# Second block of a two-block forward pass: attention head by head over both streams, with the transform branch's merge units between its steps

## The reference, cut to what matters

```python
u = ada_norm(h, g_mix[l], sh2, sc2)                       # both streams
z_conv, z_cq, z_ckv, z_kr, z_four = split_mixing(u @ w_in[l])
attn = attend(q_lat, concat(k_ctx, k_lat), concat(v_ctx, v_lat))   # 8 heads, QK 96, V 64
attn_c = attend(q_ctx, k_ctx, v_ctx)                      # context stream, not in the last layer
g0, g1, g2 = split(sigmoid(u @ w_bgate + b_bgate), 3)
y = (g0 * (silu(layer_norm(conv31(z_conv))) @ w_pw + b_pw)    # convolution branch
     + g1 * (attn @ w_o_mla)                                  # attention branch
     + g2 * (fft_real(z_four) @ w_fourier + b_four)) @ w_out  # transform branch
```

## Time and profile before

| | us |
|---|---|
| median of 3 runs | 3125.01 |
| lowest to highest | 3124.36 to 3130.96 |
| the profiled execution: its time | 3125.91 |
| the profiled execution: its span | 3124.2 |

### The profile page before, as it was taken

One profiled execution on the slowest core, in us unless ns is written; L12 is line 12 of the kernel. 1 busy time (PEld: TensorE's weight loads), 2 busy tenths in 40 slices (PEclk: granted clock), 3 DMA queues, 4 the chain that ended last, 5 costly groups with the idle time before them and its releaser, 6 DMA issues.

```text
span 3124.2 us, 52116 instructions
## 1 busy us (share of the span) xinstructions
PE 2976.0 (95%) x19700; PEld 2676.8 (86%) x19700; DVE 2058.4 (66%) x3303; ACT 1372.9 (44%) x2222; POOL 139.1 (4%) x205
## 2 busy tenths in 40 slices
PE   8998998998999999999889999999999999889898
PEld 8888998887999988897568898888988889769898
DVE  4657785557777777768843365767667666775655
ACT  4554444454545432354542254222542225654444
POOL 0000000000000000010000020100201002000000
PEclk9999999998999999999899999999999999999999
DMA  6434674435665565451102344545545445215454
GB/s 230 138 108 166 233 232 156 143 104 165 203 211 181 194 219 191 168 182 57 57 30 92 105 161 157 196 151 178 177 154 204 151 150 164 89 52 191 154 185 145
DMA packets 147696, 486.16 MB, mean 156 GB/s; under 512 B 16320, under 2 KB 25792, under 8 KB 147392
## 3 DMA queue, kind: packets, MB, share of 16 engines
q1 hardware_dynamic: 126640, 407.22, 39.3%
q0 software_dynamic: 20880, 76.56, 7.1%
HBM read 482.66 MB, written 1.05 MB: 155 GB/s over the span
## 4 chain that ended last, share of the span: by engine, by line
PE 77%; DVE 12%; ACT 5%; issue 4%; DMA 2%; DVEq 0%; POOLq 0%; ACTq 0%; SPq 0%
PE bank L1795 22%; PE bank L1797 21%; PE bank L1796 21%; DVE wlo L1018 4%; ACT whi L542 3%; PE bank L1739 2%; PE bank L1740 2%; PE bank L1741 2%; DVE acc L1542 2%; DMA bbb<-in_w_ada 1%; PE bank L2012 1%; PE aux L1996 1%; DVE bbb L1088 1%; PE bank L1870 1%; DVE small L1557 1%
## 5 line engine op out<-in xcount | busy, mean ns | idle before, releaser
L1018 DVE TENSOR_TENSOR wlo<-raw,whi 128x1024 fp32r<-128x1024 f32 (+4 forms) x850 | 948.1, 1118 | 500.2 <-ACT whi L542 494.5
L1795 PE MATMUL bank<-uhi,whi 128*128 128x256 f32 (+1 forms) x4000 | 1246.9, 312 | 13.0 <-DVE wlo L1018 6.2
L1796 PE MATMUL bank<-ulo,whi 128*128 128x256 f32 (+1 forms) x4000 | 1235.5, 309 | 0.0
L1797 PE MATMUL bank<-uhi,wlo 128*128 128x256 f32 (+1 forms) x4000 | 1235.2, 309 | 0.0
L542 ACT CAST whi<-raw 128x1024 fp32r<-128x1024 f32 (+4 forms) x850 | 810.5, 961 | 308.5 <-PE bank L1797 213.1
L1795 PEld LDWEIGHTS bank<-uhi,whi 128*128 128x128 f32 x4000 | 754.8, 189 | 75.3 <-issue 19.6
L1796 PEld LDWEIGHTS bank<-ulo,whi 128*128 128x128 f32 x4000 | 755.1, 189 | 44.7 <-issue 0.2
L1797 PEld LDWEIGHTS bank<-uhi,wlo 128*128 128x128 f32 x4000 | 755.1, 189 | 44.6
L1795 PE MATMUL bank<-yhi,whi 128*128 128x256 f32 (+1 forms) x1432 | 443.9, 310 | 16.3 <-DVE wlo L1018 9.7
L1796 PE MATMUL bank<-ylo,whi 128*128 128x256 f32 (+1 forms) x1448 | 446.1, 308 | 0.0
L1797 PE MATMUL bank<-yhi,wlo 128*128 128x256 f32 (+1 forms) x1432 | 440.7, 308 | 0.0
(11 more groups left out here) (266 smaller groups left out, 2946.5 us busy)
## 6 DMA issues: line engine op xcount, KB each, us to landing
raw<-in_w_stream SPq DMA_DIRECT2D x674, 512.0 KB, 3.5
big<-in_w_ada POOLq DMA_DIRECT2D x64, 512.0 KB, 3.9
vt<-in_w_ada POOLq DMA_DIRECT2D x51, 512.0 KB, 3.7
raw<-in_w_stream SPq DMA_DIRECT2D x80, 256.0 KB, 2.8
raw<-in_w_stream SPq DMA_DIRECT2D x48, 384.0 KB, 3.2
bbb<-in_w_ada POOLq DMA_DIRECT2D x29, 512.0 KB, 4.5
raw<-in_w_stream SPq DMA_DIRECT2D x32, 192.0 KB, 2.6
raw<-in_w_stream SPq DMA_DIRECT2D x16, 128.0 KB, 2.0
```

The lines of the kernel that those rows point to most:

```text
L1018: ve.tensor_tensor(wlo[:, u % SLOTS, 0:n], raw[:, u % SLOTS, 0:n], whi[:, u % SLOTS, 0:n].bitcast(F32), ALU.subtract).then_inc(s_low, 1)
L1795: te.matmul(out_, whi[:, u % SLOTS, w], hi(k)[:, c0:c1], start=k == 0, stop=False)
L1796: te.matmul(out_, whi[:, u % SLOTS, w], lo(k)[:, c0:c1], start=False, stop=False)
L1797: ins = te.matmul(out_, wlo[:, u % SLOTS, w], hi(k)[:, c0:c1], start=False, stop=k == plan.kt[u] - 1)
```

## The change

- Attention runs once for both streams together, head by head: for each head two context steps and two latent steps in layer 0 (32 steps), two latent steps in layer 1 (16 steps). A class `Heads` keeps which step is which.
- The transform branch's 16 units of a layer (8 gates, 8 branches) leave the merge stage and become a stage `four` of their own. Gate unit m stands behind step 4(m+1) of layer 0, branch unit m behind step 4(m+1)+2; in layer 1 behind steps 2(m+1) and 2(m+1)+1. Those that would lie past the end stand behind the last step, which are the last two in either layer. The units use banks 0 and 1 in turn.
- So attention's outputs gather in bank 2 alone, now for both streams of two heads, and the split is taken once for them. Scores have two banks in place of three and run two steps ahead in place of three.
- The gate of the transform branch is made as 0.5 tanh(0.5 x + 0.5 b) + 0.5, with Tanh on ScalarE and the rest on VectorE, where the other gates keep Sigmoid. The half bias is made once a layer (`half_bias`).
- The merge stage has 32 units of the two other branches, and its last addition takes the transform branch from `big1`.
- The norm of the convolution is at steps 23 and 9 of the new count; its Silu and the split of its output stand behind the last step instead of beside one. The table of the exponential is loaded ahead of the `kv` stage instead of behind `q`.

```diff
-LN_AT = [6, 8]
+LN_AT = [23, 9]
...
-        out.append((f"bm{l}", [8, 4, 8, 4, 8, CT] * DT))
+        out.append((f"four{l}", [8, 4] * DT))
+        out.append((f"bm{l}", [8, 4, 8, CT] * DT))
...
+class Heads:
+    def __init__(self, l):
+        self.streams = (0, 1) if l < L - 1 else (1,)
+        self.per = QT * len(self.streams)
+        self.steps = H * self.per
+        self.places = {}
+        for m in range(DT):
+            first = self.per * (m + 1)
+            self.places[2 * m] = first
+            self.places[2 * m + 1] = min(first + self.per // 2, self.steps)
+    def at(self, n):
+        return n // self.per, self.streams[n % self.per // QT], n % QT
+    def units_at(self, n):
+        return [k for k, at in self.places.items() if at == n]
+    def closes(self, n):
+        return n and n % (2 * self.per) == 0
...
# ScalarE
+                def gate4(k):
+                    if k % 2 == 0:
+                        m = k // 2
+                        done(u4, k, 0, 0)
+                        if k == 0:
+                            act.wait_ge(s_hbias, l + 1)
+                        sc.activation(big1[:, m, c0:T2], pair(u4, k)[:, c0:T2], ACT.Tanh, bias=half_bias[:, m:m + 1],
+                                      scale=0.5).then_inc(read(u4, k), 1)
                 for n in range(N + 1):
                     if n < N:
-                        turned.wait(1)
-                        sc.copy(pp[:, 2 + n % 2, 0:nk], banks[6 + n % 2][:, 0:nk]).then_inc(s_pt, 1)
+                        turned2(n)
+                    for k in heads.units_at(n - 1):
+                        gate4(k)
                     if n + 2 < N:
                         exp(n + 2)
-                    if n and n % 4 == 0:
+                    if heads.closes(n):
                         head.wait(1)
-                        j = n // 4 - 1
-                        sc.copy(yhi[:, j, s * S:(s + 1) * S], banks[j % 2][:, 0:S]).then_inc(s_ahi, 1)
+                        j = n // (2 * heads.per) - 1
+                        sc.copy(yhi[:, j, c0:T2], banks[2][:, c0:T2]).then_inc(s_ahi, 1)
+                    for k in heads.units_at(n - 1):
+                        high(u4 + k + AHEAD)
...
+                sc.preload_act_table(ACT.Exp)
                 u0 = U[f"kv{l}"]
...
# VectorE
+                def branch4(k):
+                    if k % 2:
+                        m = k // 2
+                        dve.wait_ge(*after(u4 + k - 1))
+                        chained(ve.tensor_scalar(big1[:, m, c0:T2], big1[:, m, c0:T2], 0.5, 0.5, ALU.mult, ALU.add))
+                        done(u4, k, 0, 0)
+                        ve.scalar_tensor_tensor(big1[:, m, c0:T2], banks[(u4 + k) % 2][:, c0:T2], b_four[:, m:m + 1],
+                                                big1[:, m, c0:T2], ALU.add, ALU.mult).then_inc(read(u4, k), 1)
...
-                    if n + 3 < N:
-                        bias(n + 3)
-                    if n and n % 4 == 0:
+                    if n + 2 < N:
+                        bias(n + 2)
+                    for k in heads.units_at(n - 1):
+                        branch4(k)
+                    if heads.closes(n):
                         ahi.wait(1)
-                        j = n // 4 - 1
-                        rest(ylo[:, j, s * S:(s + 1) * S], banks[j % 2][:, 0:S], yhi[:, j, s * S:(s + 1) * S])
-                    if not s:
-                        conv.taps(1)
-                        continue
+                        j = n // (2 * heads.per) - 1
+                        rest(ylo[:, j, c0:T2], banks[2][:, c0:T2], yhi[:, j, c0:T2])
+                    for k in heads.units_at(n - 1):
+                        low(u4 + k + AHEAD)
...
# TensorE
-                    if n + 3 < N:
-                        scores(n + 3)
+                    if n + 2 < N:
+                        scores(n + 2)
...
+                    for k in heads.units_at(n):
+                        unit4(k)
-                split.wait(2)
+                split.wait(1)
```

More of the change, by code:

```diff
@@ L456, in _ @@
             for name, n in plan.count.items():
-                per = 12 if name.startswith("bm") else SLOTS
+                per = 8 if name.startswith("bm") else SLOTS
                 first = SLOTS if U[name] == 0 else 0
@@ L879, in attention2 @@
                         sc.preload_act_table(ACT.Exp)
[L880 to L887, removed]
+                for k in heads.units_at(N):
+                    gate4(k)
+                    high(u4 + k + AHEAD)
+                lng, lnb = p2("ln_g", l, CT), p2("ln_b", l, CT)
+                sc.preload_act_table(ACT.Silu)
+                for m in range(CT):
+                    act.wait_ge(s_scaled, CT * l + m + 1)
+                    sc.activation(ychi[:, m, c0:T2], acc[:, m, c0:T2], ACT.Silu, bias=lnb[:, m:m + 1],
+                                  scale=lng[:, m:m + 1])
+                    sc.activation(acc[:, m, c0:T2], acc[:, m, c0:T2], ACT.Silu, bias=lnb[:, m:m + 1],
+                                  scale=lng[:, m:m + 1]).then_inc(s_chigh, 1)
             for l in range(L):
@@ L2011, in outputs, with unit4 @@
                     for k in range(nk // P):
-                        ins = te.matmul(banks[hh // 2 % 2][r, qt * P:(qt + 1) * P], vt[:, k, hh * HD:(hh + 1) * HD],
+                        ins = te.matmul(banks[2][r, q0:q0 + P], vt[:, k, hh * HD:(hh + 1) * HD],
                                         pp[:, 2 + n % 2, k * P:(k + 1) * P], start=k == 0, stop=k == nk // P - 1)
-                    if n % 4 == 3:
+                    if heads.closes(n + 1):
                         ins.then_inc(s_head, 1)
-                for n in range(3):
+                def unit4(k):
+                    gate = k % 2 == 0
+                    unit(u4, k, 0, 0, lambda t: uhi[:, t, :] if gate else yhi[:, FG + t, :],
+                         lambda t: ulo[:, t, :] if gate else ylo[:, FG + t, :], c0, T2, True)
+                for n in range(2):
                     scores(n)
@@ L2029, in attention2 @@
                         ins.then_inc(s_cmean, 1)
[L2030 removed]
+                    if n == LN_AT[l] + 3:
                         for m in range(CT):
@@ L2106, in _ @@
                 aop.wait(1)
-                for s in range(c0 // S, 2):
-                    attention2(l, s)
-                rows_of = {1: (yhi, ylo, 0), 3: (yhi, ylo, 4)}
+                attention2(l)
+                pe.wait_ge(*after(U[f"bm{l}"] - 2))
                 def rows(part):
                     def at(j, k):
-                        if j % 6 == 5:
+                        if j == 1 and part == 0 and k == 0:
+                            pe.wait_ge(*after(U[f"bm{l}"] - 1))
+                        if j % 4 == 3:
                             if part == 0 and k == 0:
```

123 lines of the change are left out of this document (67 added, 56 removed).

## The result

The changed kernel takes **3071.6 us** (median of 4 runs, 3064.2 to 3086.1) against 3124.75 for the kernel before in the same comparison: a ratio of 0.9831, interval 0.9810 to 0.9852. The forecast was 3111 with a range of 3099 to 3122. The direction was right; the gain of 53 us is nearly four times the forecast of 14, and outside the range.

What follows compares the result with a forecast made beforehand. Attention was taken as a latency chain with holes, the merge stage as matmul-bound. Gains of 18.6 - 2.5 - 1.2 - 0.4 = 14.5 us, off 3125.9, gave 3111, range 3099 to 3122.

Steps and rivals of the forecast that it cites:

- the hole time: Attention stages: the change fills TensorE's idle gaps with merge units, and can win only those gaps; units' own time cancels.
- What else moves: Side effects: table load costs 1.2 us in layer 0 and 0.4 in layer 1; Tanh, weight DMAs and queues cost nothing.
- to the first transpose: Layer 0, start of attention: from the first scores to TensorE's first transpose, 4.2 us instead of 4.4.
- first four steps: Layer 0, attention steps with no unit behind them, run at the lower clock: 12.0 us.
- pass between kinds of matmul: Both layers' attention: TensorE going between attention's and a unit's matmuls and back costs 0.2 us per unit, 3.2 per layer.
- ring and norm: Layer 0 attention: VectorE and ScalarE's probability chain is late 0.2 to 0.4 us once a head; with norm, 4.0 in all.
- ring, steps 3 to 8, layer 1: VectorE and ScalarE wait on each other longer than TensorE's step while taps last: 1.0 us a step, 5.7 in all.
- seam at the merge stage's start, layer 1: Convolution's Silu, with two table loads, stands ahead of the fourth unit's conversion: about 1.0 us lost.
- moved table load: Exponential's table load, now ahead of the key and value units, comes late: 1.2 us in layer 0, 0.4 in layer 1.
- the holes close fully: Rival: no chain stalls or switching cost in either layer, gain 33 us, so 3092; chance 0.13.
- the ring reaches layer 0 too: Rival: layer 0's 14 steps with a unit each lose layer 1's 1.0 us, giving 3121; chance 0.12.
- the slower rival: Rival: attention's small matmuls between units hold TensorE's clock down, up to 3166 over layer 0 behind step 4; chance 0.05.

Runs made afterwards that it cites:

- the kernel with the bias moved: Changed kernel with `half_bias` allocated behind all other second-block tiles, so every other tile lies where it did before the change: 3107.6 us, ratio 0.9941.
- the second kernel at each: Kernel before with, at 32, weights and rows all 32 bytes further: ratio 1.0001; at 96, 32 bytes behind the weights and 32 ahead of the rows: 0.9994.

## Why the prediction was wrong, and where it was right

**The step that failed is a missing one.** The account went through the instructions and put at nothing a line of the change that issues none: the allocation of `half_bias`, which the diff in "The change" leaves out too. The prediction says "What it can win is the hole time, not the units' time", and "they cost the same in both places, so they cancel", with 0.235 and 0.119 us per matmul taken as constants of the kernel. They are constants of a placement. With the rows 32 bytes further, all unit matmuls of the program follow one another faster, from a mean of 0.1207 us to 0.1189 for 256 columns and from 0.2343 to 0.2333 for 512, moved or not. 34 us of the measured 53 came from there. Also "What else moves" looked at queues, tables and DMAs, and never at addresses.

**The other steps,** against the kernel with the bias moved, in which that effect is absent. Its 3107.6 us lie 3 from the forecast and inside the range. In part that is luck: the layers gained 24.8 us by the traces where 16.1 were forecast, while the table's load in layer 1 cost 0.9 more than forecast. By the medians of one session the reordering gives 19.5 us, against the 14.5 of the sum.

| term | forecast, us | measured |
|---|---|---|
| layer 0, attention and units | 150.1 | 145.7 |
| of it: to the first transpose | 4.2 | 4.1 |
| of it: first four steps | 12.0 | 11.4 |
| of it: pass between kinds of matmul | 3.2 | 0.8 |
| of it: ring and norm | 4.0 | 0.5 + 1.4 |
| layer 0's gain | 18.6 | 297.7 - 274.8 = 22.9 |
| layer 1, attention and units | 92.8 | 88.5 |
| of it: ring, steps 3 to 8, layer 1 | 5.7 | 4.9 |
| of it: pass between kinds of matmul | 3.2 | about 0 |
| seam at the merge stage's start, layer 1 | 1.0, at the fourth unit | 0.4 + 0.65 idle, at the fourth and fifth |
| layer 1's gain | -2.5 | 156.7 - 154.8 = 1.9 |
| moved table load | 1.2 + 0.4 | 1.3 + 1.3 |

(The gains take attention and merge stage together, from the first scores to the merge stage's end.)

The mis-sized term in both layers is the **pass** between attention's matmuls and a unit's: 0.2 us each, from one place of the first block. In layer 0 of the kernel with the bias moved, the transposes that open two successive heads stand 16.33 us apart:

```profile
1553.78 0.38 PE L2069 MATMUL aux<-cst,pp 128*128 128x128 f32 x2
...
1570.11 0.38 PE L2069 MATMUL aux<-cst,pp 128*128 128x128 f32 x2
```

36 unit matmuls at 0.2343 are 8.43 of them, and the four steps 7.90, where I had 7.8 for the steps alone: 0.05 for each of the two units instead of 0.2, as far as the 7.8 holds, in which a context step's 1.4 is an estimate. What the earlier trace rows show, a first matmul that follows late, is made up at the other end: in layer 1 a unit starts 0.56 us behind the start of the scores ahead of it, where transposes start 0.97 behind theirs (2772.60 to 2773.57 us in the kernel before), and the transposes behind a unit come late by as much. One interval is not a cost, a whole period is. In layer 1 a step with a gate unit took 5.33 us and one with a branch unit 3.93, together 9.26; 2 x 2.51 and 36 x 0.1178 are 9.26 too.

In layer 0 the **ring** was held to cost 4.0 and costs 1.9: 0.5 at the second head, and 1.4 at the last step, which the profiles of all the kernels with the new order show. There VectorE waits for the high half as in layer 1, and the norm's three multiplications stand between the low half and the probabilities:

```profile
1644.88 0.69 DVE L1069 TENSOR_TENSOR wlo<-raw,whi 128x512 fp32r<-128x512 f32 x1 [1.35 <-ACT whi L569]
1645.48 1.89 DVE L1659 TENSOR_TENSOR acc<-acc,spare 128x512 f32<-128x512 f32 x3
...
1648.03 0.66 PE L2069 MATMUL aux<-cst,pp 128*128 128x128 f32 x4 [1.40 <-DVE pp L1618]
```

The forecast had such a wait ("a few tenths to 2 us once"). Its other part, 0.2 to 0.4 once a head from the sum of eight durations, was within that sum's error. In layer 1 the ring was rightly found and placed, but not in all its effects: of TensorE's idle time in steps 3 to 8, 1.8 us are transposes that wait for probabilities, and 1.9 are outputs that wait for the split of two heads (0.43 and 1.44), which the forecast had not named. Both go when the taps move. Measured, two steps of VectorE took 11.25 and 10.98 us there, 5.55 each, against the 5.9 of the forecast; and the 4.9 of the table are what TensorE's steps 3 to 8 take beyond the 5.33 and 3.93 us of steps without a wait.

Of the rivals, "the holes close fully" is nearer for layer 0 than the forecast was; "the ring reaches layer 0 too" is wrong; the clock rose before the first unit and stayed, so the slower rival did not come up. The range failed because its width came from the terms that were in the sum.

## What to carry to other kernels

Read the allocations in a diff as part of the change: a tile of 32 bytes moved every tile behind it and was worth more than the reordering. When a changed kernel is compared, look first at a stretch whose code is the same in both traces; if that moved, split the change before explaining it. And when two engines form a ring, put the work that needs neither partner into the wait: here moving four taps ahead of one wait closed 5.1 us.

## What the hardware showed that I had not expected

The mean spacing of these unit matmuls depends on the distance between the weights' and the rows' addresses, at four distances 32 bytes apart, named by their place modulo 128: for 256 columns 0.1207 us at 32 and 96 (0.1209 and 0.1208 in the second kernel at each), 0.1174 to 0.1189 at 64, 0.1223 at 0; for 512 columns 0.2343, 0.2333, 0.2333 and 0.2268 at 32, 64, 96 and 0. At 64 two rates alternate by stretches. A quicker matmul does not pay in full, by one profile of each: against the kernel with the bias moved, the changed one spends 31.1 us less on matmuls and 11.0 more on waits.

Left open: why; what chooses between 0.1133 and 0.1178 in a stretch; whether the effect repeats every 128 bytes; distances finer than 32 bytes; and whether a kernel with 64 in the first block and 0 in the stages of 512 columns would gain from both, which was not tried.
